# FFN up projection: one 512-column matmul for the high weights against both parts of h, with the low part added afterwards

## The chip, the cores and the metric

The kernel runs on one core of a Trainium2 chip. The metric is the device time of one execution in microseconds, as the median of three runs. TensorE (PE) multiplies, VectorE (DVE), ScalarE (ACT) and GpSimd (POOL) work element by element, and SyncE (SP) issues the weight transfers.

## The reference

Two transformer blocks on 256 tokens of width 2048, one after the other. Both contain a feed-forward network of width 5632: an up projection to value and gate (2 x 5632 columns), a depthwise convolution of width 3 over the tokens, SiLU of the gate times the value, and a down projection. Block 1 in its essentials (the second block convolves around the token instead of causally, and has the same sizes):

```python
def conv_glu_ffn(h, w_up, conv_w, conv_b, w_down):
    S = h.shape[1]
    u = h @ w_up
    up = jnp.pad(u, ((0, 0), (CONV_WIDTH - 1, 0), (0, 0)))
    u = sum(conv_w[j] * up[:, j:j + S] for j in range(CONV_WIDTH)) + conv_b
    val, gate = jnp.split(u, 2, axis=-1)
    return (jax.nn.silu(gate) * val) @ w_down
```

All of it is float32. The kernel gets that accuracy from a faster matrix format by splitting both factors into a high and a low part, and summing three products: high weights times high h, low weights times high h, high weights times low h.

## The kernel before

**Tiling of the up projection.** h stands in SBUF as 16 tiles of 128 channels x 256 tokens, in two tensors: `mhi` (high part) and `mlo` (low part). Weights come from memory in slabs of 128 x 1024: two channel tiles (`kk`) of 512 output columns. A slab is transferred into `raw` (a ring of four), ACT rounds it to the high part `whi` (function `hi`, line L1847), and the low part is `wlo = raw - whi`: POOL does the even slabs (L1831), DVE the odd ones (`lo2`, recorded as L2498). Both rings have four places as well, and `hi` of slab n waits until PE is done with slab n-4.

**Turns.** For each block there are 11 turns. A turn makes 512 value columns from slabs 0 to 7 (the value half) and 512 gate columns from slabs 8 to 15 (the gate half). That makes 2 x 11 x 16 = 352 slabs. In a slab, `slab` goes over two channel tiles and four blocks of 128 columns (`j`), and `product` issues three matmuls of 256 columns for each: 24 matmuls, each with its own weight load. The sums stand in PSUM, two 256-column blocks in a bank: the value in banks 2 and 3, the gate in banks 0 and 1.

**What follows a half.** When the last slab of a half is done (semaphore `slab_used`), ACT makes four taps (`fn`, L1850: PSUM times a convolution weight plus bias, into SBUF) and then DVE makes eight more (`stt`, L2506). Each engine executes its instructions in program order, and the order around the end of a half is written out by hand:

```python
# ACT, each half of a turn: hi of the slabs up to index 2 of the next half, then
act.wait_ge(sem.slab_used, n1 + (half + 1) * GS + more * step)
for j in range(4):
    ins = fn(tiles(11 + half)[:, j, :], u[:, j, :], ACT.Identity, ...)
# after a value half, hi of slab index 3 of the gate half comes next in the queue
# after a gate half: hi of slab index 3 of the next turn, then a wait for DVE's taps, SiLU,
# and hi of slab index 4
# DVE, each half: lo2 and the ada products, then
dve.wait_ge((sem.val_tap, sem.gate_tap)[half], NFF * b + done + 1 + i)
# eight stt, and only then lo2 of slab index 3 of the next half
```

So the low part of the fourth slab of each half (index 3) stands behind the taps of the half before it, on ACT and on DVE. After a gate half, SiLU and the product of value and gate stand there too, then a copy of the next convolution weights (L2740), and then the low part of the slab with index 5.

DVE has other work besides: the modulation vectors of later stages, summed in quarters (`piece`, L2506 and L2502) between the splits. There are two such units in each turn of block 1, one in each of eight turns of block 2 and none in its last three. When a unit is complete, PE adds up its partitions with a few one-column matmuls (`finish`), at the end of a half where a turn has two units.

Of the kernel before, what the change touches and what calls it, by code (L numbers as in the profile page):

```python
# [28 lines left out]
P = 128  # L29
# [209 lines left out]
class Semaphores:  # L239


    def __init__(self, nc, ctx):
# [66 lines left out]
        self.lo2_ready = new("lo2_ready")  # L309
        self.lo_ready = new("lo_ready")  # L310
# [81 lines left out]
def build(nc, wstream, adastream, x_in, cols_in, conv_in, tabs_in, rw_in, wg_in, out):  # L392
    ctx = ExitStack()
    with ctx:  # L394
# [20 lines left out]
        hi_h, _ = sb("hi_h", [P, KT * S + 128], F32R)  # L415
        lo_h, _ = sb("lo_h", [P, KT * S + 128], F32R)
        hhi, mhi = (hi_h[:, a:a + KT * S].rearrange("p (k s) -> p k s", s=S) for a in (0, 32))
        hlo, mlo = (lo_h[:, a:a + KT * S].rearrange("p (k s) -> p k s", s=S) for a in (0, 32))
# [78 lines left out]
        def last_place(p, j):  # L497
            return pair(p)[:, j, :] if j < 3 else bank[5][:, 0:S]

# [1344 lines left out]
        def _(act):  # L1844
# [102 lines left out]
            def ffn(n0, b):  # L1947
# [41 lines left out]
            def down(n0, b, more):  # L1989
# [3 lines left out]
                for half in range(2):  # L1993
                    kk0 = NFF * half
                    if half == 1:

                        for g, p in enumerate((1, 0)):
# [72 lines left out]
        def _(pe):  # L2070
# [15 lines left out]
            def slab(n, p, rh, rl, first, last, per=0, i=0, kks=(0, 1), tile=None, own=False):  # L2086
# [3 lines left out]
                for kk in kks:  # L2090
                    if tile is not None:
                        pe.wait_ge(sem.h_ready, tile + kk + 1)
                    for j in range(4):
# [7 lines left out]
                        if kk == 1 and j == 3:  # L2101
                            ins.then_inc(sem.slab_used, 1)

# [204 lines left out]
            def up(n0, b, h0, segments):  # L2308
# [4 lines left out]
                def body(t, i, per, units):  # L2313
                    late = i is None and t == 0 and units == 2
                    for half in range(2):
                        p = 1 - half
                        free = (sem.free_val, sem.free_gate)[half]
                        if i is None and t == 0:
                            pe.wait_ge(*st["free"][p])
                        else:  # L2320
                            pe.wait_ge(free, gb + t + (0 if i is None else i))
# [21 lines left out]
            def down(n0, b, N, x0, units):  # L2343

                def piece(kk, half, g, n, per=0, i=0, first=False, last=False):

                    p = ((1, 0), (2, 1))[half][g]
                    pe.wait_ge(sem.gs_lo, 2 * NFF * b + kk + 1 + (per // 4) * i)
                    if first and half == 0:
                        pe.wait_ge((sem.free_gate, sem.free_val)[p], NFF * (b + 1))  # L2350
                    if first and half == 1 and p == 1:
                        pe.wait_ge(sem.down_out, 6 * b + 1)
# [139 lines left out]
        def _(dve):  # L2492
# [234 lines left out]
            def ffn(n0, b, segments):  # L2727
# [3 lines left out]
                for turns, units, own in segments:  # L2731
                    u0 = st["unit"]
                    first, last = done == 0, done == NFF - 1
                    with at.loop(dve, turns, {sem.lo2_ready: GS - first, sem.gs_lo: 2 * last, sem.cw_ready: 1, sem.free_val: 1, sem.free_gate: 1,
# [3 lines left out]
                        for half in range(2):  # L2738
# [30 lines left out]

                            dve.wait_ge((sem.val_tap, sem.gate_tap)[half], NFF * b + done + 1 + i)  # L2770
                            u, t = pair(1 - half), tiles(11 + half)
                            marks = []
                            for j in range(4):
                                c = 16 * half + 4 * j
                                stt(t[:, j, 1:S], u[:, j, 0:S - 1], cw[:, c + 1:c + 2],
                                                 t[:, j, 1:S], ALU.mult, ALU.add).then_inc(*at.up(sem.step))
                                marks.append(at.last)
                            for j in range(4):
# [3 lines left out]
                                stt(t[:, j, o], u[:, j, f], cw[:, c + 2:c + 3], t[:, j, o], ALU.mult, ALU.add).then_inc(*at.up((sem.free_val, sem.free_gate)[half] if j == 3 else sem.step))  # L2782
# [249 lines left out]
```

## Time and profile before

| | us |
|---|---|
| Median of three runs | 2483.61 (2482.77 to 2484.79) |
| The profiled execution | 2484.13 |
| Its span in the trace | 2482.3 |
| PE busy | 2439.5 (98%) |
| DVE busy | 1543.8 (62%) |
| POOL busy | 1233.1 (50%) |
| ACT busy | 1126.7 (45%) |

The span is the time from the first to the last recorded instruction. Matmuls are pipelined, so a record lasts longer than the distance to the next one; the distance between starts says what a matmul costs.

### The profile page before, as it was taken

Reading aid. Unit: us, or ns where it says so; the run is one execution under the profiler, and the core shown is the slowest. Engines: PE = TensorE matmul, PEld = TensorE weight load, DVE = VectorE, ACT = ScalarE, POOL = GpSimd, SP = SyncE. Lnnn points to the kernel's source line nnn. Section 1 sums busy time; section 2 is a strip of 40 time slices with the busy share of each in tenths; the row PEclk is TensorE's granted clock in tenths of the full one; section 3 lists DMA queues with packets and bytes.
Section 4 is the critical chain, followed back from the end, with each engine's and each line's share of the span. In section 5 each row is a group of like instructions: output and inputs, shape, how many; then the busy total and the mean of one; then the engine's idle time right before and its main releaser. Section 6 shows DMA issues by size and latency. Waiting matters only on the chain.

```text
span 2482.3 us, 49449 instructions
## 1 busy us (share of the span) xinstructions
PE 2439.5 (98%) x19158; PEld 2252.9 (91%) x19158; DVE 1543.8 (62%) x2638; ACT 1126.7 (45%) x1343; POOL 1233.1 (50%) x502
## 2 busy tenths in 40 slices
PE   6999999999999999999999999999999999999998
PEld 5797997999999999998888988999999999998886
DVE  2537667666867767776666778566657655453333
ACT  2254324444444444444444544444444444454444
POOL 2574445775444444454444676575444434444443
PEclk8999999999999999999999999999999999999999
DMA  9974565797787777777776666586665665556553
GB/s 392 395 267 182 201 225 217 265 356 254 274 284 259 269 283 261 270 269 278 261 280 236 248 240 251 185 312 231 217 258 204 226 246 194 181 176 203 189 192 127
DMA packets 140524, 611.63 MB, mean 246 GB/s; under 512 B 15600, under 2 KB 15984, under 8 KB 115824
## 3 DMA queue, kind: packets, MB, share of 16 engines
q1 hardware_dynamic: 140112, 609.09, 67.4%
q8 instruction: 90, 1.47, 0.2%
q10 hardware_dynamic: 288, 0.79, 0.1%
q14 instruction: 34, 0.28, 0.0%
HBM read 607.72 MB, written 2.10 MB: 246 GB/s over the span
## 4 chain that ended last, share of the span: by engine, by line
issue 67%; POOL 30%; POOLq 1%; DMA 1%; ACT 0%
POOL wlo L1831 30%; DMA raw<-wstream 1%; POOLq L1828 1%; POOLq L1830 0%; POOLq L394 0%; ACT whi L1847 0%; POOL xT L1838 0%; POOLq L1831 0%; ACT hi_h L1847 0%; POOLq L3024 0%
## 5 line engine op out<-in xcount | busy, mean ns | idle before, releaser
L1831 POOL TENSOR_TENSOR wlo<-raw,whi 128x1024 fp32r<-128x1024 f32 x496 | 1229.4, 2484 | 1226.8 <-ACT whi L1847 1226.1
L1847 ACT ACTIVATE whi<-raw 128x1024 fp32r<-128x1024 f32 x760 | 800.6, 1059 | 922.4 <-PE psum L2074 756.5
L2074 PE MATMUL psum<-hi_h,whi 128*128 128x256 f32 x4224 | 1207.7, 286 | 5.1 <-issue 1.6
L2074 PE MATMUL psum<-hi_h,wlo 128*128 128x256 f32 x4224 | 1191.7, 282 | 0.0
L2074 PE MATMUL psum<-lo_h,whi 128*128 128x256 f32 x4224 | 1191.3, 282 | 0.0
L2074 PEld LDWEIGHTS psum<-hi_h,whi 128*128 128x128 f32 x4224 | 800.2, 189 | 18.8 <-issue 9.6
L2074 PEld LDWEIGHTS psum<-hi_h,wlo 128*128 128x128 f32 x4224 | 800.5, 190 | 0.8 <-issue 0.5
L2074 PEld LDWEIGHTS psum<-lo_h,whi 128*128 128x128 f32 x4224 | 799.9, 189 | 0.0
L2498 DVE TENSOR_TENSOR wlo<-raw,whi 128x1024 fp32r<-128x1024 f32 x264 | 390.2, 1482 | 274.8 <-ACT whi L1847 274.8
L2506 DVE SCALAR_TENSOR_TENSOR psum<-ada_raw,cact,psum 128x256 f32<-128x256 f32 x996 | 431.5, 483 | 25.6 <-DMA ada_raw<-adastream 15.4
L2074 PE MATMUL psum<-whi,gshi 128*128 128x512 f32 x704 | 276.4, 393 | 0.3 <-DVE wlo L2498 0.3
L2074 PE MATMUL psum<-wlo,gshi 128*128 128x512 f32 x704 | 274.2, 389 | 0.0
L2074 PE MATMUL psum<-whi,gslo 128*128 128x512 f32 x704 | 274.1, 389 | 0.0
L2506 DVE SCALAR_TENSOR_TENSOR arena<-psum,cw,arena 128x255 f32<-128x255 f32 (+1 forms) x352 | 141.4, 475 | 153.6 <-ACT arena L1850 153.6
L2074 PEld LDWEIGHTS psum<-whi,gshi 128*128 128x128 f32 x704 | 132.2, 188 | 29.5 <-issue 1.9
L2074 PEld LDWEIGHTS psum<-wlo,gshi 128*128 128x128 f32 x704 | 132.1, 188 | 27.9
L2074 PEld LDWEIGHTS psum<-whi,gslo 128*128 128x128 f32 x704 | 132.2, 188 | 26.7
L2498 DVE TENSOR_TENSOR gslo<-arena,gshi 128x1024 fp32r<-128x1024 f32 x44 | 56.7, 1292 | 111.3 <-ACT gshi L1847 111.3
L1850 ACT ACTIVATE arena<-psum,cw 128x256 f32<-128x256 f32 x176 | 84.9, 563 | 77.6 <-PE psum L2074 77.6
L2074 PE MATMUL psum<-whi,hi_h 128*128 128x512 f32 x224 | 92.9, 415 | 0.0
L2074 PE MATMUL psum<-wlo,hi_h 128*128 128x512 f32 x224 | 87.7, 392 | 0.0
L2074 PE MATMUL psum<-whi,lo_h 128*128 128x512 f32 x224 | 87.5, 391 | 0.0
(175 smaller groups left out, 1508.0 us busy)
## 6 DMA issues: line engine op xcount, KB each, us to landing
raw<-wstream SPq DMA_DIRECT2D x760, 512.0 KB, 4.5
ada_raw<-adastream SPq DMA_DIRECT2D x168, 1024.0 KB, 6.8
arena<-adastream SPq DMA_DIRECT2D x24, 1024.0 KB, 17.9
xT<-x_in SPq DMA_DIRECT2D x8, 512.0 KB, 7.4
gs_pages<-tabs_in SPq DMA_DIRECT2D x2, 512.0 KB, 4.3
gs_pages<-rw_in SPq DMA_DIRECT2D x2, 512.0 KB, 7.1
y_out<-xT SPq DMA_DIRECT2D x2, 512.0 KB, 3.2
y_out<-xT ACTq DMA_DIRECT2D x1, 512.0 KB, 2.8
```

The source lines that it names most:

```text
L1828: with pool.Fori(0, (n1 - n0) // RING) as i:
L1831: nc.gpsimd.tensor_tensor(wlo[:, q, :], raw[:, q, :], whi[:, q, :].bitcast(F32), ALU.subtract).then_inc(sem.lo_ready, 1)
L1847: return nc.scalar.activation(out_, in_, ACT.Copy, scale=scale)
L1850: return nc.scalar.activation(out_, in_, f, **kw)
L2074: return nc.tensor.matmul(o, lhsT, rhs, start=start, stop=stop, skip_group_check=True)
L2498: return V.tensor_tensor(o, a, b, op_)
L2506: return V.scalar_tensor_tensor(out=o, in0=a, scalar=s, in1=b, op0=op0, op1=op1)
```

## The change

The two parts of h become two halves of one tensor (`h_parts`), so that a matmul can take both: 2 x 256 = 512 columns. For each channel tile and block, one 512-column matmul multiplies the high weights with both parts of h, and one of 256 columns multiplies the low weights with the high part. The two results of the first stand side by side in one bank: in the left half the sum of the high product and the low-weight product, in the right half the product with h's low part. The right half has to be added to the left one after the last slab.

Four blocks now fill four banks in each half, and value and gate together need eight where only seven are free (bank 7 serves the modulation sums). They share bank 3: it holds block 3 of both. Block 3 of a half therefore comes a slab later in the first two slabs: PE does blocks 0 to 2 of slab 0, blocks 0 to 2 of slab 1, then waits for bank 3 (`low_added`), and does block 3 of slab 0 and of slab 1. The use of slab 0 is thus reported near the end of slab 1.

At the end of a half, ACT first copies the four right halves to SBUF (`low_out`). DVE then adds block 3 and moves it into the emptied right half of another bank (first add, which frees bank 3), and adds blocks 0 to 2 (second add). The four taps of ACT wait for both adds, and the rest follows as before. The down projection takes its first two banks in the other order.

```diff
-        hi_h, _ = sb("hi_h", [P, KT * S + 128], F32R)
-        lo_h, _ = sb("lo_h", [P, KT * S + 128], F32R)
+        h_parts, _ = sb("h_parts", [P, 2, KT * S + 128], F32R)
+        hh, mh = (h_parts[:, :, a:a + KT * S].rearrange("p x (k s) -> p x k s", s=S) for a in (0, 32))
+        hhi, hlo, mhi, mlo = hh[:, 0], hh[:, 1], mh[:, 0], mh[:, 1]
...
+        def up_bank(half, j):
+            return 3 + (j + 1) % 4 if half else j
+        def up_place(half, j):
+            return bank[up_bank(half, j)][:, 0:S] if j < 3 else bank[up_bank(half, 0)][:, S:2 * S]
+        def up_first(half):
+            return psum[:, up_bank(half, 0):up_bank(half, 0) + 3, 0:S]
+        def up_low(half, j, n=1):
+            return tiles(13 + half)[:, up_bank(half, j) - 3 * half:up_bank(half, j) - 3 * half + n, :]
...
# ACT, ffn
                         act.wait_ge(sem.slab_used, n1 + (half + 1) * GS + more * step)
+                        copy(tiles(13 + half), psum[:, 3 * half:3 * half + 4, S:2 * S]).then_inc(sem.low_out, 1)
                         if half == 0:
                             act.wait_ge(sem.cw_ready, gb + 1 + t + step)
-                        u = pair(1 - half)
+                        act.wait_ge(sem.low_added, 4 * (gb + t) + 2 * half + 2 + 4 * step)
                         for j in range(4):
                             c = 16 * half + 4 * j
-                            ins = fn(tiles(11 + half)[:, j, :], u[:, j, :], ACT.Identity,
+                            ins = fn(tiles(11 + half)[:, j, :], up_place(half, j), ACT.Identity,
                                      scale=cw[:, c:c + 1], bias=cw[:, c + 3:c + 4])
...
# PE
+            def up_block(n, half, k, j, kks=(0, 1)):
+                q = n % RING
+                o = bank[up_bank(half, j)]
+                for kk in kks:
+                    kt = 2 * k + kk
+                    w = slice(kk * 512 + j * P, kk * 512 + (j + 1) * P)
+                    mm(o.rearrange("p (x s) -> p x s", x=2), whi[:, q, w], mh[:, :, kt, :], kt == 0, kt == KT - 1)
+                    ins = mm(o[:, 0:S], wlo[:, q, w], mhi[:, kt, :], False, kt == KT - 1)
+                return ins
...
-                            slab(n0 + 2 * GS * t + half * GS + k, p, mhi[:, 2 * k:2 * k + 2, :],
-                                 mlo[:, 2 * k:2 * k + 2, :], k == 0, k == GS - 1, 2 * GS * per, 0 if i is None else i,
-                                 tile=h0 + 2 * k if i is None and t == 0 and half == 0 else None)
+                            n = n0 + 2 * GS * t + half * GS + k
+                            ready(n, 2 * GS * per, step)
...
+                            for j in range(3):
+                                up_block(n, half, k, j)
+                            if k == 1:
+                                if half:
+                                    pe.wait_ge(sem.low_added, 4 * (gb + t) + 1 + 4 * step)
+                                else:
+                                    pe.wait_ge(sem.low_added, 4 * (gb + t) - 1 + 4 * step)
+                                up_block(n - 1, half, 0, 3).then_inc(sem.slab_used, 1)
+                            if k:
+                                up_block(n, half, k, 3).then_inc(sem.slab_used, 1)
...
# DVE, ffn
+                            dve.wait_ge(sem.low_out, 2 * (NFF * b + done) + half + 1 + 2 * i)
+                            tt(up_place(half, 3).unsqueeze(1), bank[3][:, 0:S].unsqueeze(1), up_low(half, 3), ALU.add
+                               ).then_inc(*at.up(sem.low_added))
+                            tt(up_first(half), up_first(half), up_low(half, 0, 3), ALU.add).then_inc(*at.up(sem.low_added))
                             dve.wait_ge((sem.val_tap, sem.gate_tap)[half], NFF * b + done + 1 + i)
```

In the first half of the first turn of a block, whose tiles of h are only being made, the order within a slab stays as it was.

## Rows read from the trace of the kernel before

**Rows 1.** The page: busy time, share and instructions of PE.

```profile
PE 2439.5 (98%) x19158; PEld 2252.9 (91%) x19158; DVE 1543.8 (62%) x2638; ACT 1126.7 (45%) x1343; POOL 1233.1 (50%) x502
```

**Rows 2.** Windows, up stage of block 1: window, length, busy by engine, clock, DMA.

```profile
640.00:1130.00 490.00, 490.00 (x4076) 487.36 (x4075) 359.92 (x646) 231.00 (x269) 222.44 (x86) 1.00 0.76 271
```

**Rows 3.** Timeline of PE, up: start, duration, instruction; first and last of 53.

```profile
799.73 0.28 PE L2074 MATMUL psum<-lo_h,whi 128*128 128x256 f32 x1
...
805.90 0.28 PE L2074 MATMUL psum<-hi_h,whi 128*128 128x256 f32 x1
```

**Rows 4.** Timeline of PE, down stage: first and last of 28.

```profile
1199.80 0.39 PE L2074 MATMUL psum<-whi,gshi 128*128 128x512 f32 x1
...
1205.92 0.39 PE L2074 MATMUL psum<-whi,gshi 128*128 128x512 f32 x1
```

**Rows 5.** Timeline of PE between a value half and the gate half behind it.

```profile
812.31 0.50 PE L2074 MATMUL psum<-tabs,acc 128*128 128x1 f32 x4
812.67 0.37 PE L2074 MATMUL psum<-hi_h,whi 128*128 128x256 f32 x1
```

**Rows 6.** Timeline of ACT: ends of the value and the gate half.

```profile
812.59 1.93 ACT L1850 ACTIVATE arena<-psum,cw 128x256 f32<-128x256 f32 x4 [1.86 <-PE psum L2074]
814.40 1.07 ACT L1847 ACTIVATE whi<-raw 128x1024 fp32r<-128x1024 f32 x1
815.79 1.06 ACT L1847 ACTIVATE whi<-raw 128x1024 fp32r<-128x1024 f32 x1 [0.33 <-PE psum L2074]
...
835.73 1.93 ACT L1850 ACTIVATE arena<-psum,cw 128x256 f32<-128x256 f32 x4 [1.78 <-PE psum L2074]
...
840.94 1.06 ACT L1850 ACTIVATE arena<-arena 128x1024 f32<-128x1024 f32 x1 [2.33 <-DVE arena L2506]
841.90 1.99 ACT L1847 ACTIVATE whi<-raw 128x1024 fp32r<-128x1024 f32 x2
```

**Rows 7.** Timeline of DVE in the same stretch.

```profile
814.55 3.21 DVE L2506 SCALAR_TENSOR_TENSOR arena<-psum,cw,arena 128x255 f32<-128x255 f32 x8 [3.39 <-ACT arena L1850]
817.68 2.73 DVE L2498 TENSOR_TENSOR wlo<-raw,whi 128x1024 fp32r<-128x1024 f32 x1
...
840.82 1.22 DVE L2498 TENSOR_TENSOR wlo<-raw,whi 128x1024 fp32r<-128x1024 f32 x1
...
845.67 1.21 DVE L2498 TENSOR_TENSOR wlo<-raw,whi 128x1024 fp32r<-128x1024 f32 x1
```

**Rows 8.** Timeline of POOL in the same stretch.

```profile
816.93 2.40 POOL L1831 TENSOR_TENSOR wlo<-raw,whi 128x1024 fp32r<-128x1024 f32 x1 [3.76 <-ACT whi L1847]
...
843.03 2.62 POOL L1831 TENSOR_TENSOR wlo<-raw,whi 128x1024 fp32r<-128x1024 f32 x1 [6.64 <-ACT whi L1847]
845.85 3.29 POOL L1831 TENSOR_TENSOR wlo<-raw,whi 128x1024 fp32r<-128x1024 f32 x1 [0.20 <-ACT whi L1847]
```

**Rows 9.** Timeline of DVE after a gate half of block 2.

```profile
2051.25 3.41 DVE L2498 TENSOR_TENSOR wlo<-raw,whi 128x1024 fp32r<-128x1024 f32 x1
```

**Rows 10.** Timeline of POOL there.

```profile
2048.61 4.97 POOL L1831 TENSOR_TENSOR wlo<-raw,whi 128x1024 fp32r<-128x1024 f32 x2 [6.63 <-ACT whi L1847]
```

**Rows 11.** Groups by shape: count, busy us, mean ns, idle before.

```profile
L2498 DVE TENSOR_TENSOR acc<-acc,psum 128x256 f32<-128x256 f32 x54 | 22.7, 421 | 1.9
...
L2498 DVE TENSOR_TENSOR arena<-arena,psum 128x512 f32<-128x512 f32 x16 | 11.0, 687 | 17.4 <-PE psum L2074 17.4
...
L1847 ACT ACTIVATE arena<-psum 128x1024 f32<-128x1024 f32 x10 | 10.2, 1017 | 7.2 <-PE psum L2074 7.2
```

**Rows 12.** The page: weight transfers, KB each, median us to landing.

```profile
raw<-wstream SPq DMA_DIRECT2D x760, 512.0 KB, 4.5
```

**Rows 13.** Windows of 4 us around two pauses of PE: columns as before.

```profile
1610.00:1614.00 4.00, 2.42 (x21) 2.40 (x21) 3.02 (x4) 1.25 (x4) 0.00 (x0) 1.00 0.36 128
...
1622.00:1626.00 4.00, 2.34 (x20) 2.13 (x19) 3.11 (x9) 1.06 (x1) 4.00 (x3) 1.00 0.86 283
1626.00:1630.00 4.00, 4.00 (x23) 4.00 (x23) 1.29 (x4) 0.00 (x0) 3.55 (x2) 0.57 0.98 350
```

More of the change, by code:

```diff
@@ L309, in __init__ @@
         self.lo2_ready = new("lo2_ready")
+        self.low_out = new("low_out")
+        self.low_added = new("low_added")
         self.lo_ready = new("lo_ready")
@@ L1995, in down @@
                     if half == 1:
-                        for g, p in enumerate((1, 0)):
+                        for g, p in enumerate((0, 1)):
                             act.wait_ge(sem.slab_used, n0 + DOWN_HALF - 2 + 2 * g)
@@ L2315, in body @@
                     for half in range(2):
[L2316 to L2321, printed above, removed]
+                        step = 0 if i is None else i
+                        begins = i is None and t == 0
+                        if begins and half == 0:
+                            pe.wait_ge(*st["free"][0])
+                            pe.wait_ge(*st["free"][1])
+                        elif not begins:
+                            pe.wait_ge((sem.free_val, sem.free_gate)[half], gb + t + step)
                         for k in range(GS):
@@ L2326, in body @@
                                 finish(0, per, 0 if i is None else i)
-                            slab(n0 + 2 * GS * t + half * GS + k, p, mhi[:, 2 * k:2 * k + 2, :],
-                                 mlo[:, 2 * k:2 * k + 2, :], k == 0, k == GS - 1, 2 * GS * per, 0 if i is None else i,
-                                 tile=h0 + 2 * k if i is None and t == 0 and half == 0 else None)
+                            n = n0 + 2 * GS * t + half * GS + k
+                            ready(n, 2 * GS * per, step)
+                            if begins and half == 0:
+                                for kk in range(2):
+                                    pe.wait_ge(sem.h_ready, h0 + 2 * k + kk + 1)
+                                    for j in range(4):
+                                        ins = up_block(n, half, k, j, (kk,))
+                                ins.then_inc(sem.slab_used, 1)
+                                continue
+                            for j in range(3):
[8 more added lines that the diff above has]
+                                up_block(n, half, k, 3).then_inc(sem.slab_used, 1)
                         if units == 2 and not (late and half == 0):
@@ L2733, in ffn @@
                     first, last = done == 0, done == NFF - 1
-                    with at.loop(dve, turns, {sem.lo2_ready: GS - first, sem.gs_lo: 2 * last, sem.cw_ready: 1, sem.free_val: 1, sem.free_gate: 1,
+                    with at.loop(dve, turns, {sem.lo2_ready: GS - first, sem.gs_lo: 2 * last, sem.cw_ready: 1, sem.free_val: 1, sem.free_gate: 1, sem.low_added: 4,
                                                 sem.g_made: 1, sem.acc_ready: units, sem.ada_used: units,
@@ L2774, in ffn @@
                                 c = 16 * half + 4 * j
-                                stt(t[:, j, 1:S], u[:, j, 0:S - 1], cw[:, c + 1:c + 2],
+                                stt(t[:, j, 1:S], up_place(half, j)[:, 0:S - 1], cw[:, c + 1:c + 2],
                                                  t[:, j, 1:S], ALU.mult, ALU.add).then_inc(*at.up(sem.step))
@@ L2781, in ffn @@
                                 o, f = (slice(2, S), slice(0, S - 2)) if b == 0 else (slice(0, S - 1), slice(1, S))
-                                stt(t[:, j, o], u[:, j, f], cw[:, c + 2:c + 3], t[:, j, o], ALU.mult, ALU.add).then_inc(*at.up((sem.free_val, sem.free_gate)[half] if j == 3 else sem.step))
+                                stt(t[:, j, o], up_place(half, j)[:, f], cw[:, c + 2:c + 3], t[:, j, o], ALU.mult, ALU.add).then_inc(*at.up((sem.free_val, sem.free_gate)[half] if j == 3 else sem.step))
                         lo2(n1 + 2 * GS + 3, 2 * GS, i)
```

12 lines of the change are left out of this document (6 added, 6 removed).

## The prediction, made before the changed kernel ran

> **What bounds the kernel now.** I read the page first: PE is busy for 98% of the span [rows 1]. An average over stages says little of one stage, so I took the windows next: in the up stage of block 1 PE is busy for all of its 490 us, at a granted clock of 1.00, while DVE, ACT and POOL are busy for 73%, 47% and 45% [rows 2]. So the matmul stream sets the time there, and every other engine only has to deliver each slab's low weights before PE comes to it. The timeline of PE then prices the stream. Starts of 256-column matmuls lie (805.90 - 799.73) / 52 = 118.65 ns apart [rows 3]; starts of 512-column matmuls in the down stage (1205.92 - 1199.80) / 27 = 226.7 ns [rows 4]. A slab is 24 x 118.65 = 2.848 us. A half is 8 slabs and 0.36 us of one-column matmuls [rows 5], 23.14 us in all, the distance between the two groups of taps [rows 6].
>
> The last view is the timelines of ACT, DVE and POOL around the ends of halves, because the change works there. Let T be the start of the taps. PE begins the next half at T + 0.08 [rows 5, 6] and wants its fourth slab (index 3) 3 x 2.848 us later, at T + 8.62. After a value half DVE makes that slab's low part from T + 5.09 to T + 7.82 [rows 7]: it comes 0.8 us early. It took 2.73 us and not 1.2 because POOL was splitting a slab, from T + 4.34 to T + 6.74, and DVE ended 1.08 us after POOL [rows 7, 8]. After a gate half the fourth slab is ready at T + 6.31, the fifth (POOL) at T + 9.92 and the sixth (DVE) at T + 11.15 [rows 7, 8]; PE wants them at 8.62, 11.47 and 14.32. The slack is 0.8 to 3.2 us, and all of it hangs on a queue that starts at T.
>
> **The change, part by part.**
>
> *Matmuls.* Three of 256 columns (355.95 ns) become one of 512 and one of 256 (226.7 + 118.65 = 345.3 ns). That is 10.6 ns for each of 8 groups in a slab, 0.085 us a slab (2.763 us is left), and 30.0 us over 352 slabs. What is saved is the fixed part of one matmul and its weight load. The trace shows no 512-column matmul among 256-column ones, nor one whose columns come in two runs. The bounds: nothing, if it costs 237.3 ns like two of 256, and twice this, if the 256-column matmul behind it loses its fixed part too (108 ns, by the slope of 108 ns for 256 columns). I take 10.6, which both rows give.
>
> The Trainium skill, "TensorE: Matmul & The Clock Gate", section "Back-to-back issue gap", puts the fixed part of a matmul at about 2.5 ns, 109 ns for 256 columns. The row shows 118.65 ns, so the trace does not agree. By the page's figure the change would save only some 7 us, and the time forecast below would be an estimated 2542 us instead of 2531.
>
> *Work ahead of the taps.* The ACT copy of 128 x 1024 out of PSUM costs 1.02 us [rows 11]. The first add is a 128x256 one (0.42 us; the next can start some 0.09 us before its end, as the eight stt of 3.21 us show against their single durations). The second has 768 columns: 421 ns for 256 and 687 ns for 512 [rows 11] make 1.04 ns a column and 0.95 us. With three handoffs between engines of 0.03 us, the gap between taps and stt [rows 6, 7], the taps start 1.02 + 0.33 + 0.95 + 0.09 = 2.39 us later. The lower bound is 2.1 us, with the second add at the price of 512 columns; the upper one 3.0 us, with it at three times 421 ns and handoffs of 0.1 us. DVE is free in time: it now idles from 1.4 us before T [rows 7], and by the delays below it would be done some 0.7 us after T in the busiest half, before the copy ends.
>
> *Behind the taps in ACT's queue* stand the high parts of the next slabs, in DVE's the low part of the fourth slab. All of it moves by 2.39 us.
>
> After a value half, the fourth slab's high part runs from T + 4.20 to 5.27 and the fifth's from T + 5.15 to 6.2. PE has released the fifth's place by then: slab 0 is done after 14 groups, 4.84 us into the half. POOL splits the fifth from T + 6.29 to 8.69. DVE comes to its split of the fourth at T + 7.48, meets POOL and ends 1.08 us behind it, at T + 9.77. PE wants it at 0.08 + 3 x 2.763 = 8.37 and starts 0.1 us after it is ready: a stall of 1.5 us where there was none.
>
> After a gate half POOL is idle, so DVE ends the fourth slab at 6.31 + 2.39 = T + 8.70: 0.43 us of stall. SiLU waits for the stt, the fifth's high part for SiLU [rows 6], and POOL ends the fifth at 9.92 + 2.39 = T + 12.31; PE wants it at 8.80 + 2.76 = 11.56: 0.85 us. For the sixth slab it matters who comes first. Before, DVE began at T + 9.94, just ahead of POOL [rows 7, 8]. Now PE is late, so the seventh slab's high part is there long before POOL is done with the fifth, and POOL goes on at once. One turn of block 2 shows this case: POOL's two splits end at 2053.58, DVE's at 2054.66, again 1.08 us later [rows 9, 10]. The sixth is then ready at 12.31 + 2.40 + 1.08 = T + 15.79, wanted at 12.41 + 2.76 = 15.17: 0.72 us. Together 2.0 us.
>
> *Covered.* Block 3's wait for bank 3 asks for the first add, done at T + 1.5, and PE comes to it 12 groups (4.1 us) into the half. The weight transfers wait for splits four slabs back: the late fourth slab's place is refilled by T + 9.77 + 4.5 = 14.3 [rows 12], and PE wants the slab in it, index 7, at T + 20.9. Modulation transfers stand in the same SP queue, and move with DVE's products, with more room still. The other order of banks in the down stage moves one wait to results that are there earlier.
>
> *The sum.* 3.5 us of stalls a turn x 22 turns = 77 us, less 30.0 us of matmuls: +47 us. Against the profiled execution's 2484.13 us that is 2531 us; the median of the runs is 0.5 us below it, which changes nothing. Where the chain is 0.1 us longer or shorter, both halves of 22 turns move: 4.4 us, so its bounds give 2518 to 2558. The matmul's bounds give 2516 to 2546, because between T and the last stall PE's own speed doesn't count and only 8 of 16 slabs profit.
>
> **The rivals.**
>
> *Faster: the chain stays hidden.* If the copy and adds cost no more than the slack, only the 30 us remain: 2454 us. For it speaks that ACT and DVE are idle for much of the stage [rows 2]. Against it: the smallest slack is 0.8 us, 0.55 once PE is faster, and the copy alone takes 1.02 us. It decides at a turn's stalls of 30 / 22 = 1.36 us; below that the kernel is faster. Chance 0.08.
>
> *Slower by little: DVE and POOL do not meet.* If DVE gets the fourth slab's split in before POOL, and the sixth's too, the value half loses 0.43 us and the gate half 1.28: 1.71 x 22 - 30 = +8 us, 2492 us. For it: in the gate half of the rows DVE won. Chance 0.12.
>
> *Slower by more: PE's clock falls at the new pauses.* A pause of 1.66 us at 1623 was followed by a window at a granted clock of 0.57; one of 1.58 us at 1610 was not [rows 13]. At half clock, 0.43 x 4 = 1.7 us are lost each time. If all 22 value-half pauses of 1.5 us did this, that would be 38 us more: 2569 us. Against it: they lie in an unbroken stream and are shorter than both. Chance 0.16.
>
> **How the numbers follow.** The forecast, stalls in both halves at an unchanged clock, has a chance of 0.64, and its own range is 2512 to 2558. The range for all is 2490 to 2574: it leaves out the faster case, the edge of the little-slower one and what lies beyond the clock case. A measurement of this kernel tells 0.2%, 5 us, from no change. Slower by more than that: the forecast, the clock case and most of the 2492 us case, 0.87. Within it: 0.05, the lower part of that case. Faster: 0.08.
>
> **What the changed profile would show.** PE: in the up stage no longer 100% busy but 92 to 95%, with pauses ended by the low weights of DVE and POOL, at the fourth slab after each value half, and at the fourth, fifth and sixth after each gate half. Between pauses, 226.7 and 118.65 ns between starts. ACT: 44 copies of about 1.0 us, with the taps some 2.4 us after the copy's start. DVE: adds of about 0.42 and 0.95 us; the fourth slab's split ends near T + 9.8 (T now the copy's start) after a value half and near T + 8.7 after a gate half. The prediction is wrong if PE doesn't pause there, if the adds or the copy are much cheaper, if a 512-column matmul with two runs costs far from 227 ns, or if the granted clock in the stage falls.

## The result, and the profile after

The changed kernel takes 2546.82 us (median of 4 runs, 2546.03 to 2551.61) against 2483.19 us before: a ratio of 1.0262, 95% interval 1.0244 to 1.028. It is slower by 64 us. The forecast was 2531 us, so the direction holds and the size is short by 16 us. The profiled execution took 2546.03 us, with a span of 2544.2 us, 62 us above the one before.

The page: busy time of PE [rows 1].

```profile
PE 2447.2 (96%) x16342; PEld 2115.3 (83%) x16342; DVE 1644.3 (65%) x2726; ACT 1166.6 (46%) x1387; POOL 1236.9 (49%) x502
```

Windows of the up stages of block 1 and block 2; columns as in [rows 2].

```profile
670.00:1140.00 470.00, 449.25 (x2531) 385.15 (x2530) 377.76 (x635) 223.83 (x260) 195.57 (x77) 1.00 0.70 256
1835.00:2290.00 455.00, 433.94 (x2427) 372.30 (x2426) 279.41 (x389) 218.41 (x255) 188.87 (x75) 1.00 0.56 203
```

PE is busy for 449.25 of 470 us (95.6%) and 433.94 of 455 us (95.4%), where it had been busy for all of block 1's stage [rows 2]; 92 to 95% were forecast. The granted clock is 1.00 in both.

What ended PE's pauses, block 1: us in total, times, longest. The records of matmuls overlap, so the pauses look shorter here than the delay that they cause.

```profile
PE psum L2092 <- DVE wlo L2547: 9.5, 14, 1.3
PE psum L2092 <- DVE acc L2547: 6.4, 10, 0.8
PE psum L2092 <- POOL wlo L1848: 4.9, 9, 0.6
```

The first such line of block 2, where the longest pauses are:

```profile
PE psum L2092 <- DVE wlo L2547: 16.2, 24, 1.6
```

The low weights of DVE and of POOL were expected. The wait for `acc`, in block 1 alone, was not: that is the sum of the modulation unit, for which PE's one-column matmuls stand between the value and the gate half.

Groups by shape (count, busy us, mean ns, idle before): the new work ahead of the taps. The 54 copies include the 10 that the kernel before had [rows 11].

```profile
L1864 ACT ACTIVATE arena<-psum 128x1024 f32<-128x1024 f32 x54 | 55.3, 1024 | 78.1 <-PE psum L2092 78.1
...
L2547 DVE TENSOR_TENSOR psum<-psum,arena 128x768 f32<-128x768 f32 x44 | 42.1, 956 | 0.0
...
L2547 DVE TENSOR_TENSOR psum<-psum,arena 128x256 f32<-128x256 f32 x44 | 19.0, 432 | 87.7 <-ACT arena L1864 87.6
```

The timelines of the turn that [rows 5 to 8] showed. ACT, from the end of its value half to the start of the next turn:

```profile
821.44 1.02 ACT L1864 ACTIVATE arena<-psum 128x1024 f32<-128x1024 f32 x1 [1.74 <-PE psum L2092]
823.83 1.93 ACT L1867 ACTIVATE arena<-psum,cw 128x256 f32<-128x256 f32 x4 [1.36 <-DVE psum L2547]
825.65 1.07 ACT L1864 ACTIVATE whi<-raw 128x1024 fp32r<-128x1024 f32 x1
827.61 2.01 ACT L1864 ACTIVATE whi<-raw 128x1024 fp32r<-128x1024 f32 x2 [0.90 <-PE psum L2092]
...
846.63 1.03 ACT L1864 ACTIVATE arena<-psum 128x1024 f32<-128x1024 f32 x1 [1.75 <-PE psum L2092]
849.03 1.93 ACT L1867 ACTIVATE arena<-psum,cw 128x256 f32<-128x256 f32 x4 [1.37 <-DVE psum L2547]
```

DVE there:

```profile
821.48 0.42 DVE L2547 TENSOR_TENSOR acc<-acc,psum 128x256 f32<-128x256 f32 x1
822.50 1.30 DVE L2547 TENSOR_TENSOR psum<-psum,arena 128x256 f32<-128x256 f32 x2 [0.60 <-ACT arena L1864]
825.80 3.21 DVE L2555 SCALAR_TENSOR_TENSOR arena<-psum,cw,arena 128x255 f32<-128x255 f32 x8 [2.00 <-ACT arena L1867]
828.93 3.30 DVE L2547 TENSOR_TENSOR wlo<-raw,whi 128x1024 fp32r<-128x1024 f32 x1
...
854.12 1.22 DVE L2547 TENSOR_TENSOR wlo<-raw,whi 128x1024 fp32r<-128x1024 f32 x1
...
858.97 3.42 DVE L2547 TENSOR_TENSOR wlo<-raw,whi 128x1024 fp32r<-128x1024 f32 x1
```

POOL there:

```profile
828.75 2.40 POOL L1848 TENSOR_TENSOR wlo<-raw,whi 128x1024 fp32r<-128x1024 f32 x1 [6.58 <-ACT whi L1864]
...
856.33 4.97 POOL L1848 TENSOR_TENSOR wlo<-raw,whi 128x1024 fp32r<-128x1024 f32 x2 [8.97 <-ACT whi L1864]
```

PE after the value half (two starts), and the first and last of 23 starts in the unbroken stream behind it:

```profile
821.95 0.61 PE L2092 MATMUL psum<-tabs,acc 128*128 128x1 f32 x4 [0.55 <-DVE acc L2547]
...
832.29 0.50 PE L2092 MATMUL psum<-h_parts,whi 128*128 128x512 f32 x1 [1.20 <-DVE wlo L2547]
...
833.79 0.39 PE L2092 MATMUL psum<-h_parts,whi 128*128 128x512 f32 x1
...
837.65 0.40 PE L2092 MATMUL psum<-h_parts,whi 128*128 128x512 f32 x1
```

Below, what a half "takes" is the distance from its taps to the taps of the next half, with the stalls that stand between. Read the gate half first, with T = 846.63, the start of its copy. The taps start at T + 2.40. DVE ends the fourth slab's split at 855.34, T + 8.71. POOL's two splits run from 856.33 to 861.30, and DVE, which comes to the sixth slab in the meantime, ends at 862.39: 1.09 us after POOL, T + 15.76. Forecast were 2.39, 8.70 and 15.79.

The value half has T = 821.44 and the taps again at T + 2.39. But PE's one-column matmuls begin only at 821.95, because DVE's sum ended at 821.90. PE enters the gate half some 0.9 us late, frees slab 0 late, and the fifth slab's high part runs at 827.61 instead of T + 5.15. POOL is still the first, by 0.18 us (828.75 against 828.93), and DVE ends at 832.23, T + 10.8 instead of 9.77. The taps are then 849.03 - 823.83 = 25.2 us apart. In 6 of block 1's 11 turns DVE wins this race. One of them, DVE, POOL and PE:

```profile
683.64 1.22 DVE L2547 TENSOR_TENSOR wlo<-raw,whi 128x1024 fp32r<-128x1024 f32 x1
```

```profile
683.61 6.86 POOL L1848 TENSOR_TENSOR wlo<-raw,whi 128x1024 fp32r<-128x1024 f32 x2 [6.62 <-ACT whi L1864]
```

```profile
676.82 0.61 PE L2092 MATMUL psum<-tabs,acc 128*128 128x1 f32 x4 [0.70 <-DVE acc L2547]
```

Here DVE's split ends at 684.86, 0.91 us before PE comes to that slab (685.77), POOL's two take 6.86 us together instead of 4.97, and PE's only pause is the one for `acc`. Such halves take 23.8 to 24.0 us. In block 2, with one unit a turn and no such sum at that place, PE's pause is the forecast one (copy at 1872.25, PE goes on at T + 9.84), and the value half takes 24.2 us:

```profile
1882.09 0.50 PE L2092 MATMUL psum<-h_parts,whi 128*128 128x512 f32 x1 [1.02 <-DVE wlo L2547]
```

### The profile page after: what moved, and what is told of

Same layout as the page of the kernel before. It is cut to its first block, busy times and chain, and to the rows that moved or that the text cites. A ratio compares the mean times of both kernels' runs of the same rounds, so it can differ in the third digit from the quotient of the medians.

```text
span 2544.2 us, 44061 instructions
## 1 busy us (share of the span) xinstructions
PE 2447.2 (96%) x16342; PEld 2115.3 (83%) x16342; DVE 1644.3 (65%) x2726; ACT 1166.6 (46%) x1387; POOL 1236.9 (49%) x502
## 4 chain that ended last, share of the span: by engine, by line
issue 67%; POOL 31%; POOLq 1%; DMA 1%; ACT 0%
POOL wlo L1848 31%; DMA raw<-wstream 1%; POOLq L1845 1%; POOLq L1847 0%; POOLq L396 0%; ACT whi L1864 0%; POOL xT L1855 0%; POOLq L1848 0%; ACT h_parts L1864 0%; POOLq L3077 0%
## 5 line engine op out<-in xcount | busy, mean ns | idle before, releaser
L2092 PE MATMUL psum<-h_parts,whi 128*128 128x256 f32 (+1 forms) x5632 | 1542.5, 343 | 50.9 <-DVE wlo L2547 34.0
L2092 PE MATMUL psum<-h_parts,wlo 128*128 128x256 f32 x4224 | 1194.5, 283 | 0.0
L2092 PEld LDWEIGHTS psum<-h_parts,whi 128*128 128x128 f32 x5632 | 975.6, 190 | 205.6 <-DVE wlo L2547 51.6
L2092 PEld LDWEIGHTS psum<-h_parts,wlo 128*128 128x128 f32 x4224 | 799.9, 189 | 0.8 <-issue 0.5
L2547 DVE TENSOR_TENSOR wlo<-raw,whi 128x1024 fp32r<-128x1024 f32 x264 | 431.6, 1639 | 221.6 <-ACT whi L1864 221.0
L1864 ACT ACTIVATE arena<-psum 128x1024 f32<-128x1024 f32 (+5 forms) x112 | 79.5, 729 | 185.5 <-PE psum L2092 181.9
L2092 PE MATMUL psum<-whi,h_parts 128*128 128x512 f32 x448 | 144.0, 403 | 0.0
L2547 DVE TENSOR_TENSOR psum<-psum,arena 128x256 f32<-128x256 f32 x88 | 57.0, 694 | 87.7 <-ACT arena L1864 87.6
L2092 PEld LDWEIGHTS psum<-whi,h_parts 128*128 128x128 f32 x448 | 81.4, 188 | 18.1 <-issue 1.3
L2092 PE MATMUL psum<-wlo,h_parts 128*128 128x512 f32 x224 | 87.7, 392 | 0.0
```

Of the source, the lines that this page charges most:

```text
L1864: return nc.scalar.activation(out_, in_, ACT.Copy, scale=scale)
L2092: return nc.tensor.matmul(o, lhsT, rhs, start=start, stop=stop, skip_group_check=True)
L2547: return V.tensor_tensor(o, a, b, op_)
```

## The experiments

Times are medians against the kernel before in the same comparison; "distance" is the time between two groups of taps, value to gate / gate to value.

**1. The chain alone, in the kernel before.** An unused copy and two adds are put ahead of its taps; matmuls, banks and releases stay.

```diff
                         act.wait_ge(sem.slab_used, n1 + (half + 1) * GS + more * step)
+                        copy(page(13 + half), flat(1 - half)).then_inc(sem.low_out, 1)
...
+                        act.wait_ge(sem.low_added, 4 * (gb + t) + 2 * half + 2 + 4 * step)
...
+                            dve.wait_ge(sem.low_out, 2 * (NFF * b + done) + half + 1 + 2 * i)
+                            spare = psum[:, 4:7, :]
+                            tt(spare[:, 0, S:2 * S], spare[:, 0, S:2 * S], tiles(13 + half)[:, 3, :], ALU.add
+                               ).then_inc(*at.up(sem.low_added))
+                            tt(spare[:, :, 0:S], spare[:, :, 0:S], tiles(13 + half)[:, 0:3, :], ALU.add
+                               ).then_inc(*at.up(sem.low_added))
```

> The kernel before, with its matmuls and banks as they were, and a copy and two adds of the same sizes ahead of the taps, whose results nobody uses. Theory: a slab stays at 2.848 us, so PE wants the fourth slab at T + 8.62; value half 1.25 us of pause, gate half 0.18 + 0.76 + 0.63 us, 2.8 us a turn, 62 us: 2546 us, between 2530 and 2560. Rival (the loss is in the form of the matmuls, the sharing of bank 3 or the late release of slab 0): within 8 us of the kernel before, 2476 to 2492 us.

2553.97 against 2484.71 us, ratio 1.028 (1.0263 to 1.0297): +69 us. Distances 24.4 / 24.6. PE waits for the same three things, block 1:

```profile
PE psum L2078 <- DVE acc L2502: 5.8, 10, 0.7
PE psum L2078 <- POOL wlo L1833: 4.3, 9, 0.5
PE psum L2078 <- DVE wlo L2502: 3.1, 10, 0.3
```

The chain makes the whole loss by itself. Neither the new matmul, the shared bank nor the late release is needed for it; with the change the loss is some 6 us smaller (64 and 69).

**2. The same change, other queues.** ACT makes the high part of the next half's fourth slab between the copy and the taps, and after a gate half those of the fifth and sixth ahead of SiLU. DVE splits the fourth right after the second add, the sixth before the gate product.

```diff
                         copy(tiles(13 + half), psum[:, 3 * half:3 * half + 4, S:2 * S]).then_inc(sem.low_out, 1)
+                        if (True, True)[half]:
+                            some_hi(n1 + (half + 1) * GS + 3, more, i)
...
-                    if i is None:
-                        his(n1 + more + 3, n1 + more + 4)
-                    else:
-                        hi(n1 + more + 3, more, i)
+                    for k in (4, 5):
+                        some_hi(n1 + more + k, more, i)
...
                             tt(up_first(half), up_first(half), up_low(half, 0, 3), ALU.add).then_inc(*at.up(sem.low_added))
+                            if (True, True)[half]:
+                                lo2(n1 + (half + 1) * GS + 3, 2 * GS, i)
...
-                        lo2(n1 + 2 * GS + 3, 2 * GS, i)
+                        lo2(n1 + 2 * GS + 5, 2 * GS, i)
```

> The changed kernel with another order of queues alone: ACT makes the high part of the next half's fourth slab between the copy and the taps, DVE its low part between the second add and the stt; after a gate half ACT makes the high parts of the fifth and sixth slab before SiLU, and DVE splits the sixth before the product of value and gate. Theory (the loss is the 2.39 us chain standing ahead of these splits): PE's pauses behind the ends of halves go, and what is left is the matmul saving. Starts of a pair lie about 352 ns apart in the changed kernel where three were 356, some 0.038 us a slab, 13 us over 352 slabs: 2470 us, between 2462 and 2482. Rival (the pauses come from the sharing of bank 3 and the late release of slab 0, or DVE has no room for its work): 2525 to 2547 us.

2485.64 against 2484.71 us, ratio 1.0005 (0.9995 to 1.0014). The waits for low weights are gone; distances are 24.2 / 22.9 in block 1, 22.9 / 22.5 in block 2. One wait of PE is left, in block 1:

```profile
PE psum L2098 <- DVE acc L2553: 10.3, 10, 1.1
```

This gives back 61 us: the late splits are the loss. It missed its 2470 us by the sum that the forecast had overlooked.

**3. One half at a time.** Of experiment 2, only the value half, or only the gate half.

```diff
-                        if (True, True)[half]:
+                        if (True, False)[half]:
...
```

> The changed kernel with the queues reordered after the value half alone. Theory: the distance from value taps to gate taps falls from 23.8 to 25.3 us (24.2 in block 2) to about 23.3 (22.9), the other one stays at 24.5: some 1.2 us a turn, 26 us: 2520 us, between 2510 and 2530. Rival (one late split delays the next, so that one half alone brings nothing): over 2538 us.

```diff
-                        if (True, True)[half]:
+                        if (False, True)[half]:
...
```

> The changed kernel with the queues reordered after the gate half alone. Theory: the distance from gate taps to value taps falls from 24.5 to about 22.9 us (22.5 in block 2), the other one stays at 24 to 25: some 1.7 us a turn, 37 us: 2510 us, between 2500 and 2520. Rival as for the value half: over 2538 us.

The value half alone: 2518.21 against 2483.48 us, ratio 1.0145 (1.013 to 1.0161), 28.6 us better than the changed kernel. The gate half alone: 2506.11 us, ratio 1.0094 (1.0078 to 1.0109), 40.7 us better. The forecast's stalls were 1.5 x 22 = 33 and 2.0 x 22 = 44 us. The two gains add up to 69 us, and both edits together gave 61: they are not independent. With the gate half alone, PE's only wait in block 1 is the same as with both:

```profile
PE psum L2098 <- DVE acc L2553: 10.2, 10, 1.1
```

and the distance from value to gate taps is 24.2 us in both runs. There DVE's late split comes before POOL's in ten of the eleven turns, and PE never waits for it.

**4. The late unit sum.** Experiment 2, and PE takes up the value half's unit in the gate half, after blocks 0 to 2 of slab 0 (at `k == 1`, not two slabs in as the expectation has it).

```diff
-                            if late and half == 1 and k == 1:
-                                finish()
+                            if units == 2 and half == 1 and k == 1:
+                                finish(0, units * per, step)
...
-                        if units == 2 and not (late and half == 0):
-                            finish(0, units * per, 0 if i is None else i)
+                        if units == 2 and half == 1:
+                            finish(0, units * per, step)
```

> The run with the queues reordered in both halves, and PE adds up the value half's modulation unit two slabs into the gate half instead of at the half's end. Theory (the 1.0 us that PE waits at the end of each value half of block 1 for DVE's sum of the unit eats the matmul saving there): the wait goes, a turn of block 1 takes some 45.7 us instead of 47.1, 11 x 1.3 = 14 us below the run with the queues reordered: 2471 us, between 2464 and 2477, faster than both kernels. Rival (DVE is then late for the adds or the next split, and the pause only moves): 2480 to 2490 us.

2472.21 us (2469.18 to 2474.99, 5 runs) against 2483.48, ratio 0.9956 (0.9942 to 0.9969): faster than both kernels, by 11 us (0.4%) and by 75 us. Distances 22.9 / 22.9, then 22.9 / 22.5. The windows, block 1 and block 2, show PE busy throughout:

```profile
670.00:1100.00 430.00, 430.00 (x2479) 377.84 (x2478) 353.80 (x625) 222.71 (x257) 196.59 (x75) 1.00 0.77 275
1800.00:2200.00 400.00, 400.00 (x2289) 350.86 (x2288) 254.28 (x379) 209.25 (x243) 179.74 (x71) 1.00 0.62 214
```

ACT and DVE after a value half:

```profile
809.83 1.03 ACT L1864 ACTIVATE arena<-psum 128x1024 f32<-128x1024 f32 x1 [1.75 <-PE psum L2098]
810.75 1.05 ACT L1864 ACTIVATE whi<-raw 128x1024 fp32r<-128x1024 f32 x1
812.22 1.94 ACT L1867 ACTIVATE arena<-psum,cw 128x256 f32<-128x256 f32 x4 [0.42 <-DVE psum L2552]
```

```profile
810.89 1.30 DVE L2552 TENSOR_TENSOR psum<-psum,arena 128x256 f32<-128x256 f32 x2
812.10 1.22 DVE L2552 TENSOR_TENSOR wlo<-raw,whi 128x1024 fp32r<-128x1024 f32 x1
814.19 3.21 DVE L2560 SCALAR_TENSOR_TENSOR arena<-psum,cw,arena 128x255 f32<-128x255 f32 x8 [0.88 <-ACT arena L1867]
```

The chain is as long as ever (copy to taps 2.39 us). The high part fits into the time in which ACT would wait for the adds, DVE's split into that in which it would wait for the taps. The split ends 3.5 us after the half instead of some 10.

**5. The late unit sum alone**, in the changed kernel: the edit of experiment 4 without that of 2.

> The changed kernel, in which alone PE adds up the value half's modulation unit two slabs into the gate half. It removes PE's wait of 0.5 to 0.7 us at the end of each value half of block 1, not the late splits. Theory (the wait lies in front of a pause that the late fourth slab makes anyway): the gate half starts earlier and then waits longer for the same split, and POOL begins ahead of DVE in all turns: within 6 us of the changed kernel, 2541 to 2553 us. Rival (the wait adds to the loss in full): 11 x 0.65 = 7 us and more below it, under 2540 us.

2546.43 against 2483.76 us, ratio 1.0249 (1.0232 to 1.0266): nothing gained. Waits of PE, block 1:

```profile
PE psum L2092 <- DVE wlo L2546: 14.3, 18, 1.2
PE psum L2092 <- POOL wlo L1848: 4.8, 9, 0.6
```

The wait for `acc` has gone into the one for the split: PE starts on time, POOL's split then comes first in every turn of block 1, and the value half takes 24.4 us. The two waits lie one behind the other, and the second takes up what the first gives back.

**6. No copy, no adds.** The product with h's low part is not added; DVE only moves block 3 (256 columns, PSUM to PSUM) and the taps wait for that.

```diff
-                        copy(tiles(13 + half), psum[:, 3 * half:3 * half + 4, S:2 * S]).then_inc(sem.low_out, 1)
...
-                            tt(up_first(half), up_first(half), up_low(half, 0, 3), ALU.add).then_inc(*at.up(sem.low_added))
+                            dve.wait_ge(sem.slab_used, n1 + (half + 1) * GS + 2 * GS * i)
+                            V.tensor_copy(up_place(half, 3), bank[3][:, 0:S]).then_inc(*at.up(sem.low_added))
```

> The changed kernel without the ACT copy and without both adds; DVE only moves block 3 out of bank 3 (256 columns, PSUM to PSUM), and the taps wait for that. The product of the high weights with the low part of h is computed and left out of the result. Theory: the chain is some 0.45 us longer than before instead of 2.39, the fourth slab comes at T + 8.3 and is wanted at T + 8.5: no pauses to speak of, the matmul saving of 13 us is left, 2470 us, between 2462 and 2484. Rival (form of the matmuls, sharing of the bank, late release): over 2510 us.

2497.96 against 2484.71 us, ratio 1.0053 (1.0036 to 1.007). A miss: I had counted the move as 0.4 us, inside the slack. DVE and POOL after a half of block 2:

```profile
1852.47 0.42 DVE L2546 TENSOR_TENSOR acc<-acc,psum 128x256 f32<-128x256 f32 x1
1852.81 0.42 DVE L2819 COPY psum<-psum 128x256 f32<-128x256 f32 x1
...
1858.37 4.43 DVE L2546 TENSOR_TENSOR wlo<-raw,whi 128x1024 fp32r<-128x1024 f32 x2
```

```profile
1858.18 2.41 POOL L1848 TENSOR_TENSOR wlo<-raw,whi 128x1024 fp32r<-128x1024 f32 x1 [5.04 <-ACT whi L1864]
```

DVE is still at its unit when the half ends, so the move starts late, the taps too, and POOL is ahead by 0.19 us. Distances are 23.3 / 23.3 there, and 22.5 in the last three turns of the block, which have no unit. Before, the taps asked PE alone, and DVE could be late unnoticed; any product of DVE ahead of the taps ends that. In block 1 the wait for `acc` is there as well (10.1 us in all, 10 times).

**7. What a 512-column matmul costs here.** In the changed kernel a pair (512 and 256 columns) takes (837.65 - 833.79) / 11 = 351 ns and not the forecast 345.3. Five runs looked for the reason. The first is experiment 6 with one contiguous run of columns for the second part of h, which is other data:

```diff
-                    mm(o.rearrange("p (x s) -> p x s", x=2), whi[:, q, w], mh[:, :, kt, :], kt == 0, kt == KT - 1)
+                    mm(o.rearrange("p (x s) -> p x s", x=2), whi[:, q, w], mhi[:, 2 * k:2 * k + 2, :] if one_run else mh[:, :, kt, :], kt == 0, kt == KT - 1)
...
```

> As the run without copy and adds, and the 512 columns that the high weights multiply lie next to each other (two channel tiles of h's high part; the sums are not those of the reference), in all halves but the first of each block. Theory of two runs (a moving operand in two runs of 256 costs some 6 ns over one of 512): starts of a pair come down from 352 to about 345 ns, 0.05 us a slab, 15 to 20 us below the run without copy and adds. Rival (a 512-column matmul between matmuls of 256 costs that by itself): the two runs agree within 4 us.

2498.92 us, ratio 1.0055 (1.0038 to 1.0072); the pair still takes 351 ns. Two runs are not the cause.

The next three ran once each, on experiment 2, for the distance of starts alone: all matmuls of 512 columns, then the weights as the moving operand, then three such in another order.

```diff
-                    ins = mm(o[:, 0:S], wlo[:, q, w], mhi[:, kt, :], False, kt == KT - 1)
+                    ins = mm(o.rearrange("p (x s) -> p x s", x=2), wlo[:, q, w], mh[:, :, kt, :], False, kt == KT - 1)
```

> The run with the queues reordered in both halves, in which the low weights too are multiplied with both parts of h in 512 columns (the product of the two low parts is added to the result). It is for the distance of starts alone. Theory of mixing (a 512-column matmul costs more when one of 256 columns follows it than when one of 512 does): all starts 226 to 228 ns apart, as in the down stage, a slab 3.63 us. Rival (in this stage a 512-column matmul costs 231 to 233 ns by itself): a slab 3.70 us or more. The time itself, some 2480 + 352 x 0.83 = 2770 us by the first.

```diff
+                    row = slice(kk * 512, (kk + 1) * 512)
+                    mm(o, mhi[:, kt, 0:P], whi[:, q, row], kt == 0, kt == KT - 1)
+                    ins = mm(o, mlo[:, kt, 0:P], wlo[:, q, row], False, kt == KT - 1)
```

> The all-512 run with the operands exchanged as in the down stage: 128 tokens of h (high or low part) stand in the array, and 512 weights of the slab stream past; the sums are not those of the reference. It is for the distance of starts alone. Theory (the exchange of operands makes a 512-column matmul of the up stage 232 instead of 227 ns): 227 to 228 ns between starts, a slab 3.64 us. Rival (the stage does, with what the other engines and the transfers do in it): 232 ns, a slab 3.71 us.

```diff
+                    mm(o, mhi[:, kt, 0:P], whi[:, q, row], kt == 0, False)
+                    mm(o, mlo[:, kt, 0:P], whi[:, q, row], False, False)
+                    ins = mm(o, mhi[:, kt, 0:P], wlo[:, q, row], False, kt == KT - 1)
```

> The run with the operands exchanged, with three matmuls of 512 columns in the order of the down stage: high h with high weights, low h with high weights, high h with low weights (the sums are not those of the reference). It is for the distance of starts alone. Theory (the order matters: in the down stage two matmuls in a row stream the same columns, in the up stage never): 227 ns. Rival (something else in the up stage): 232 ns.

They took 2788.53, 2787.56 and 3441.58 us. PE in the first, first and last of 28 starts:

```profile
799.68 0.39 PE L2098 MATMUL psum<-h_parts,wlo 128*128 128x512 f32 x1
...
805.96 0.39 PE L2098 MATMUL psum<-h_parts,whi 128*128 128x512 f32 x1
```

6.28 / 27 = 232.6 ns, and as much in the other two. So it is not the mixture with 256 columns, nor which operand moves, nor the order. The last run is experiment 4 with the two channel tiles outside and the blocks inside, so that neighbours go to different banks:

```diff
-                            for j in range(3):
-                                up_block(n, half, k, j)
+                            for kk in range(2):
+                                for j in range(3):
+                                    up_block(n, half, k, j, (kk,))
```

> The fastest kernel so far (queues reordered in both halves, the unit's sum later), in which PE goes over blocks 0 to 2 for one channel tile and then for the other, so that a new bank comes after each pair and not after each second pair. Theory (a pair of matmuls waits some 5 ns where it goes on in the bank that the pair before wrote): starts of a pair come down from 351 to about 346 ns, 10 us below that kernel, 2462 us. Rival (banks have nothing to do with it): within 3 us of it, 2469 to 2475 us.

2471.57 against 2483.48 us, ratio 0.9957 (0.9942 to 0.9971), and 351 ns a pair: not the banks either. The traces also speak against the load of the other engines: in the up stage of the all-512 run (700 to 1100 us) the median distance is 231 to 232 ns whichever of ACT, DVE and POOL are at work, and in the down stage of the kernel before (1140 to 1360 us) 226 to 227 ns, while the transfers keep the DMA engines busy for 0.61 of the first stretch and 0.74 of the second. The pairs are not even: two of three in a row take 353 to 355 ns and the third 345 or 346, with one run of columns, two runs, and in either order of banks. Why 512 columns cost 231 to 233 ns in this stage (351 less 118.65 to 120 for the other matmul, and 232.6 among their own kind) and 226.7 in the down stage [rows 4], at a granted clock of 1.00 in both, stays open.

## Why the prediction was right, and where its size was off

- *What bounds the kernel*: right. The matmul stream sets the time, the slack of the low weights is under a microsecond, and experiment 1 shows that 2.4 us ahead of the taps use it up.
- *Work ahead of the taps*: right. 2.39 us forecast and measured; the second add takes 956 ns (0.95 forecast).
- *Stalls after a gate half*: right. Forecast splits at T + 8.70 and T + 15.79, measured 8.71 and 15.76, with POOL first at the sixth slab; distance 24.5 us in both. In turns 8 to 10 of block 2's 11, DVE is first there (its split takes 1.21 us), and the distance is 23.9 to 24.05 us.
- *Stalls after a value half*: right in block 2 but for two halves at its start, which stand under the sum; elsewhere PE goes on at T + 9.84 (9.77 + 0.1 forecast). In block 1 the step "DVE is free in time" failed. It counted the copy as the only one to wait for DVE. PE waits for DVE too, for the unit's sum: it ended 0.46 us after the copy began, and PE entered the next half 0.9 us late. Where DVE's split comes first all the same, such a half costs no more than forecast (23.8 to 24.0 us); where it comes behind POOL's, in 5 turns, 25.0 to 25.3. Experiment 5 shows the two waits trading places, experiment 4 what is left without both.
- *Matmuls*: mis-sized. A pair takes 351 ns instead of 345.3, so a slab saves 8 x (355.95 - 351) = 0.040 us and not 0.085: 14 us over 352 slabs, not 30. Where nothing pauses, 11 us were seen (experiment 4). The bound from below of this term, 237.3 ns for 512 columns, held.
- *The sum*: 47 us forecast, 62 measured between the two profiled executions. By the forecast a value half grows by 1.5 - 0.68 = 0.82 us and a gate half by 1.32: 22.2 us for each block's 21 distances of taps (11 and 10), and 2.6 outside. Measured: 26.6 in block 1 (488.0 to 514.55), 30.1 in block 2 (482.0 to 512.1), 5.3 outside. Block 1's excess is that of the 5 turns (5 x 1.2 us, less what other turns fell short). Of block 2's 7.9 us, 3.5 are value halves, more than half of that in the last three turns: without a unit they took 22.7 us before, and now they take the same 24.2 as the others, whose one-column matmuls (at 1877.66 in the example) lie ahead of the stall and are hidden in it. Another 2.2 us are six gate halves, which took 22.9 us before and not the forecast's 23.14, while the chain behind T is just as long and ends in the same 24.5 us; the last three give 0.7 us back. The other 2.9 us are one gate half of 27.1 us, from the taps at 1798.88 to those at 1825.97. There "DVE is free in time" failed in the forecast's own sense:

```profile
1821.25 1.03 ACT L1864 ACTIVATE arena<-psum 128x1024 f32<-128x1024 f32 x1 [2.10 <-PE psum L2092]
```

```profile
1824.65 1.29 DVE L2547 TENSOR_TENSOR psum<-psum,arena 128x256 f32<-128x256 f32 x2
```

The copy ends at 1822.28, but DVE was busy with splits and its unit until its adds began, 2.4 us later, and the taps start 4.72 us behind the copy's start instead of 2.39. The same happened in the first value half of each block (4.64 us from 625.69, 4.06 us from 1770.67); in the 41 other halves it was 2.37 to 2.43 us. The first taps of block 1 come 4.0 us later than before and those of block 2 another 2.2, which with 0.9 us gained behind the last taps makes the 5.3 outside. The matmul term's miss lies inside these shares, with at most 8 x 0.045 x 22 = 8 us, by the 8 slabs a turn that count. The shares were read off distances and starts, and not tested one by one.

The rivals: "the chain stays hidden" didn't occur. "DVE and POOL do not meet" occurred in 6 of 22 value halves, all in block 1, and there brought nothing against the forecast, since PE had waited for the sum; it occurred in 3 of 22 gate halves, those of turns 8 to 10 of block 2, for the sixth slab. "PE's clock falls" occurred once, in block 1's first turn, ahead of the windows shown above. PE had waited for the unit's sum, and the granted clock of the two windows then was 0.79 and 0.78:

```profile
629.08 0.61 PE L2092 MATMUL psum<-tabs,acc 128*128 128x1 f32 x4 [1.32 <-DVE acc L2547]
```

```profile
628.00:632.00 4.00, 2.92 (x13) 2.56 (x14) 2.20 (x5) 1.67 (x4) 0.00 (x0) 0.79 0.85 298
632.00:636.00 4.00, 4.00 (x20) 3.48 (x19) 3.70 (x9) 2.96 (x4) 0.62 (x1) 0.78 0.62 250
```

That is an estimated (0.21 + 0.22) x 4 = 1.7 us, once. At the other pauses, of up to 1.3 us in block 1 and 1.6 us in block 2, it didn't occur: the granted clock is 1.00 in both up windows.

The Trainium skill, "SBUF — State Buffer", section "Who interferes with whom", says that DVE and GpSimd share one pair of SBUF ports under an exclusive lock, and that a DVE instruction with two SBUF inputs contends with a GpSimd instruction that reads SBUF; a split is such an instruction on either engine. The trace agrees: a split of DVE that starts 0.18 us behind POOL's takes 3.30 us instead of 1.22, and ends 1.08 us after POOL's.

The Trainium skill, "TensorE: Matmul & The Clock Gate", section "Back-to-back issue gap", weighed in the prediction, gave an estimated 7 us for what the matmuls save; the page gives that fixed part for a matmul by itself. The measured spacing gives 14 and the forecast had 30: the trace lies between the two.

## What to carry to other kernels

Work put at the end of a stage cost here what stood behind it in its engines' queues, not its own microseconds. For such a change, look up when the next stage wants the first product of each of these queues, and put that product into the gaps of the new chain. Here the order of a few splits was worth 61 us, while the change with both of its repairs gains 11. When an instruction of a busy engine enters a chain that used to ask another engine alone, list everyone who waits for that engine, because lateness that cost nothing before now has a price. A spacing taken from another stage is an estimate: the same shape took 2 to 3% more here.

## What the hardware showed that was not expected

- A 512-column matmul takes 226.7 ns in the down stage and 231 to 233 ns in the up stage, whatever its neighbours, operands, order and banks, and whichever other engines are at work.
- Which of two splits comes first decides over some 2 us of DVE's: 1.22 us where DVE was first, 3.30 where POOL was. Where DVE won, POOL's two splits took 6.86 us instead of 4.97. In block 1's value halves POOL was first where its record began 0.12 us or more ahead of DVE's, and DVE was done first where the two began within 0.06 us of each other, even where POOL's record began earlier (at 683.6 by 0.03 us, at 1026.6 by 0.05).
- A pause of PE of 1.32 us in the first turn was followed by a granted clock of 0.79 and 0.78 in the windows from 628 to 636 us; pauses of up to 1.6 us later in the up stages left it at 1.00.
